# Second layer of a two-layer attention and expert kernel: where the loads of the down weights stand in the queue

## The reference

```python
def _moe(h, w_router, router_bias, w_gate, w_up, w_down):
    shp = h.shape
    hf = h.reshape(-1, shp[-1])
    combine = _route(hf, w_router, router_bias).astype(h.dtype)
    y = jnp.zeros_like(hf)
    for e in range(N_EXPERTS):
        a = jax.nn.silu(hf @ w_gate[e]) * (hf @ w_up[e])
        y = y + combine[:, e:e + 1] * (a @ w_down[e])
    return y.reshape(shp)
```

## Time and profile before

| | |
|---|---|
| median of three runs | 1684.38 us |
| the profiled execution, its own time | 1684.62 us |
| its span, first to last instruction | 1682.6 us |
| TensorE busy | 1587.2 us (94%) |
| VectorE, ScalarE, GpSimd busy | 670.0, 341.5, 123.6 us |
| mean granted clock of TensorE | 0.976 |
| SP's DMA queue: share of the 16 DMA engines over the span | 54.9% |
| bytes read and written | 362.74 and 26.80 MB |

### The profile page before, as it was taken

How to read it: one execution, slowest core, us unless ns; L and a number is a source line. 1 busy time by engine, 2 the same in 40 slices (tenths; PEclk the granted TensorE clock), 3 DMA queues, 4 the chain that set the end, 5 groups by cost and what they waited for, 6 DMA issues and landing times. The chain is left out here.

```text
span 1682.6 us, 16523 instructions
## 1 busy us (share of the span) xinstructions
PE 1587.2 (94%) x6162; PEld 751.8 (45%) x6162; DVE 670.0 (40%) x1608; ACT 341.5 (20%) x782; POOL 123.6 (7%) x193
## 2 busy tenths in 40 slices
PE   5999999999999999899999979999999989998994
PEld 2444456544444445644444434445644445333331
DVE  2430068866677733511100145307867144111113
ACT  1210078820000021110100023007710021000001
POOL 1000000200000010200000020000200100110101
PEclk9999999999999999899999989999999999998998
DMA  9812141115545461699999996222178758999995
GB/s 345 273 50 100 50 168 66 39 51 150 201 151 200 150 225 48 244 349 366 386 391 393 366 355 202 100 100 76 39 227 324 276 193 292 370 388 392 389 360 210
DMA packets 176128, 380.83 MB, mean 226 GB/s; under 512 B 24430, under 2 KB 28670, under 8 KB 175912
## 3 DMA queue, kind: packets, MB, share of 16 engines
q1 hardware_dynamic: 160768, 327.17, 54.9%
q0 software_dynamic: 14272, 50.20, 7.8%
q10 hardware_dynamic: 1008, 2.38, 0.4%
HBM read 362.74 MB, written 26.80 MB: 232 GB/s over the span
## 5 line engine op out<-in xcount | busy, mean ns | idle before, releaser
L1881 PE MATMUL bank<-ring_sb,HT_sb 128*128 128x512 f32 x672 | 298.4, 599 | 3.1 <-ACT HT_sb L847 2.5
L1988 PE MATMUL bank<-ring_sb,HT_sb 128*128 128x512 f32 x544 | 240.6, 595 | 0.0
L1881 PEld LDWEIGHTS bank<-ring_sb,HT_sb 128*128 128x128 f32 x672 | 126.8, 193 | 151.8 <-issue 150.1
L1988 PEld LDWEIGHTS bank<-ring_sb,HT_sb 128*128 128x128 f32 x544 | 102.3, 190 | 135.7 <-issue 135.7
L1992 PE MATMUL bank<-ring_sb,QR_sb 128*128 128x512 f32 x288 | 129.5, 592 | 0.0
L2153 PE MATMUL bank<-ring_sb,HT_sb 128*64 128x512 f32 x480 | 106.5, 596 | 2.8 <-DMA ring_sb<-w_e_up 2.8
L2171 PE MATMUL bank<-ring_sb,QR_sb 128*128 128x512 f32 x208 | 97.8, 626 | 6.5 <-DMA ring_sb<-w_e_down 6.5
L973 ACT ACTIVATE WK_sb<-bank 128x512 f32<-128x512 f32 x36 | 21.5, 597 | 348.6 <-PE bank L1988 348.6
L2134 PE MATMUL bank<-ring_sb,HT_sb 128*128 128x512 f32 x192 | 85.4, 598 | 2.7 <-ACT HT_sb L1007 2.7
L2177 PE MATMUL bank<-ring_sb,QR_sb 128*64 128x512 f32 x304 | 73.8, 630 | 12.6 <-DMA ring_sb<-w_e_down 10.6
L1992 PEld LDWEIGHTS bank<-ring_sb,QR_sb 128*128 128x128 f32 x288 | 54.8, 190 | 68.8 <-issue 68.8
(11 more groups left out here) (336 smaller groups left out, 1708.7 us busy)
## 6 DMA issues: line engine op xcount, KB each, us to landing
ring_sb<-w_e_down SPq DMA_DIRECT2D x32, 2048.0 KB, 17.2
ring_sb<-w_mod SPq DMA_DIRECT2D x24, 2048.0 KB, 9.4
ring_sb<-w_in SPq DMA_DIRECT2D x22, 2048.0 KB, 15.0
ring_sb<-w_e_gate SPq DMA_DIRECT2D x16, 2048.0 KB, 14.8
ring_sb<-w_e_up SPq DMA_DIRECT2D x16, 2048.0 KB, 18.9
ring_sb<-w_e_gate SPq DMA_DIRECT2D x22, 1024.0 KB, 16.4
ring_sb<-w_e_up SPq DMA_DIRECT2D x22, 1024.0 KB, 14.6
ring_sb<-w_branch SPq DMA_DIRECT2D x8, 1024.0 KB, 9.9
```

Of the source, the lines that this page charges most:

```text
L1881: ins = mm(bank[j % 4][:, :], HT[:, k, P * t:P * t + P], WR[slot][:, k], start=(k == 0), stop=(k == KD - 1))
L1988: ins = mm(bank[i % 2][:, :], HT[:, k, P * t:P * t + P], WR[wg][:, k], start=(k == 0), stop=(k == KD - 1))
```

## The change

The down weight of position q - 1 is issued directly behind the pair of position q, from q = 3 on; before, it was the down weight of q - 2, from q = 4 on. Just ahead of the last pair one down weight is issued instead of two. In the first layer both forms give the same list.

```diff
@@ -610,13 +610,11 @@
                 at = [0, 1]
                 for q in range(2, NE):
                     at.append(eng.value_load(order[0:1, q:q + 1], min_val=0, max_val=NE - 1))
-                    lag = 2 if l else 1
                     if q == NE - 1:
-                        for late in range(q - lag, q):
-                            load_expert(l, late, at[late], 2)
+                        load_expert(l, q - 1, at[q - 1], 2)
                     load_pair(l, q, at[q])
-                    if 2 * lag <= q < NE - 1:
-                        load_expert(l, q - lag, at[q - lag], 2)
+                    if 2 + l <= q < NE - 1:
+                        load_expert(l, q - 1, at[q - 1], 2)
                 load_expert(l, NE - 1, at[NE - 1], 2)
```

## The result

The changed kernel takes 1694.60 us (median of seven runs, 1691.48 to 1697.76) against 1685.65 for the kernel before in the same seven rounds (1683.24 to 1687.79). The ratio is 1.0051, 95% interval 1.0039 to 1.0063: slower by 0.5%. The forecast was 1695.4 against a before of 1684.4, +11.0; measured are +8.9 by the medians and +8.6 by the ratio. The profiled execution of the changed kernel lies 1.8 us above its median (1696.37 us, span 1694.4).

What follows compares the result with a forecast made beforehand. The stream of weights was taken to bound the second layer's experts. Hold +10.1, closed hole -3.1 and the tail's +4.1 for D15 gave +11.0 at the last product: 1684.4 + 11.0 = 1695.4 us, range 1689.5 to 1699.

Steps and rivals of the forecast that it cites:

- The bound: Second layer's experts: the full stream of weights is the limit, 388 GB/s from 1439 to 1626 us, not TensorE's waits.
- Part 1: Start of the second layer's experts: SP, held by D2 until 1436.5 us, makes the stream 3.92 MB late, +10.1 us.
- Part 2: After the start: the stream does not stand still again at later waits of SP; costed at nothing.
- The thinnest margin: D3's wait until 1451.69 us: the stream has work until 1456, 4.6 us to spare; if gone, 1 to 2 us.
- Part 3: TensorE's 16.6 us of waits on down weights go, replaced by waits elsewhere; nothing is gained.
- Part 4: The stream's hole from 1626 to 1632 us, behind D14, closes: 1.19 MB, -3.1 us.
- Part 5: Kernel's end: gathers land ahead of D15, which becomes the stream's last load, +4.1 us; last product starts +11.0 us.
- Rival (b): Tail: TensorE's clock falls after longer waits, last product 1.7 to 2.7 us later, 1697.1 to 1698.1 us; chance 0.2.
- (a): Tail: the gathers don't get ahead of D15, so the sum is +7.0, 1691.4 us; chance 0.12.
- (c): The stream stands still again, at 1451.69 us or behind a full position: 3 to 6 us more, 1698 to 1701; chance 0.08.
- (e): Whole kernel: no change, hold and hole in balance, 1684.4 us; chance 0.03.
- (d): SP's hold at the start costs nothing and the closed hole stays: 3.1 us sooner, 1681.3 us; chance 0.05.

Runs made afterwards that it cites:

- run 6: The changed kernel without the second half of the down weights of positions 6 to 9, all matmuls kept: 1685.79 us, ratio to before 1.0001.
- the first load alone: The kernel before, with only the down weight of position 2 moved ahead of the pair of position 4: 1698.07 us, ratio 1.0058.
- run 8: The kernel before, with the pairs of positions 3 and 4 issued as gate, gate, up, up: 1686.54 us, ratio 1.0002.
- run 1: The kernel before in its old order, with only SP's wait for position 0's down product added ahead of position 4's pair: 1695.94 us, ratio 1.0053.
- run 7: The changed kernel, with GpSimd's second-layer gathers held until the last up half has landed: 1692.88 us, ratio to before 1.0044.
- the switch at 6: The kernel before up to position 6's pair, then two down weights, then the changed kernel's order: 1686.00 us, ratio 0.9990.
- the switch at 5: The kernel before up to position 5, there two down weights, then the changed kernel's order: 1687.17 us, ratio 1.0000.

## Why the prediction was right

**The bound.** Right. The stream of weights bounds the second layer's experts, not TensorE: the changed kernel has TensorE 2.5 us less busy and at a higher clock in the long stretch, and it is slower. Leaving out bytes and no matmul gave 8.4 to 8.8 us back (run 6).

**Part 1, the hold of SP.** Right in mechanism and size. +10.1 was forecast. The wait alone costs between 8.9 (ratio) and 10.0 us (medians), the first load alone between 9.8 and 12.1, and the changed kernel has carried 0.32 + 5.78 = 6.10 MB by 1455 us (its windows stand below) against 9.84, so 3.74 MB or 9.6 us at 390 GB/s are missing. One claim beside it was too strong: "nothing can make it up" from 1439 on. The stream of before has some idle time up to about 1445 (run 8), and the windows show it: the lag is 3.90 MB at the end of the first (3.92 was forecast) and 3.74 at the end of the second, where the changed kernel carries 361 GB/s and before 351. The Trainium skill ("DMA: Bandwidth & Descriptors", Anatomy of one DMA) says that any wait on a semaphore happens on the issuing sequencer before dispatch, in a section on GpSimd's path; for SP's queue the windows of run 1 agree, with 12 GB/s in 16.9 us. The figure of 358 GB/s that the same page gives for a core (Specifications) is not what the rows show, 390; it is half of a stack's 716 GB/s, for two cores, and this kernel runs on one.

**Part 2, no further standstill.** Right: 390 GB/s from 1455.46 to 1626.56 in the changed kernel. The thinnest margin held: D3 goes out at 1452.17, and the share is 1.02 from 1439.46 to 1455.46. The windows of the changed kernel, cut as those of run 1:

```profile
1422.56:1439.46 16.90, 16.90 (x54) 7.46 (x54) 2.67 (x4) 1.08 (x2) 0.87 (x2) 1.00 0.07 19
1439.46:1455.46 16.00, 16.00 (x66) 6.35 (x64) 2.39 (x4) 1.19 (x2) 2.20 (x3) 1.00 1.02 361
1455.46:1626.56 171.10, 151.99 (x640) 59.08 (x638) 19.63 (x33) 14.08 (x24) 20.08 (x28) 0.97 1.04 390
```

**Part 3, the waits on down weights.** Right in that they bring nothing. Wrong in "none on down weights", which part of the text on the new profile expected: 9.4 us of waits stay with down weights, in six pieces of at most 2.1 us: TensorE has caught up with the stream and waits for most loads in turn, whichever they are.

**Part 4, the hole.** Right: 6 us x (390 - 190) = 1.2 MB, 3.1 us. In the count from P3 the deficit shrinks from 3.9 MB ahead of the hole's place to 2.7 MB behind it.

**Part 5, the tail.** The term was mis-sized and its picture partly wrong. The gathers were to land ahead of D15, and the sum for it (18 us against 28) counted their issue and left out their landing, which took 6.4 us in the kernel before. In fact the first pair's rows were waited for until 1664.9, 1.8 us ahead of D15: the gathers ran beside D15, each slower than before. How much they took from the stream ahead of the last product is seen from P3's first load to the start of that product, first before, then changed:

```profile
1403.18:1656.62 253.44, 233.42 (x961) 93.80 (x959) 33.05 (x60) 21.27 (x36) 31.76 (x43) 0.95 1.00 369
1403.66:1666.81 263.15, 233.64 (x961) 94.20 (x959) 35.25 (x63) 21.27 (x36) 31.77 (x43) 0.97 0.97 360
```

These are 93.5 and 94.7 MB: 1.2 MB more, 3 us. D15 then cost less than the 4.1 us booked: from 10.1 - 3.1 = 7.0 the start of the last product went to 9.7, so the tail's term is 2.7 (run 7, which moves the gathers back, takes 2.2 of it). The half microsecond booked for the up half, in the middle value, wasn't spent either, because D15 came last by far.

Rival (b), the fallen clock, given 0.2, came true beside it: 1.7 us at the last product, at the lower end of the 1.7 to 2.7 forecast. It struck in two places. In `up_gate(15)` it cost 2.0 us, which D15's landing hides. Before D15, where the wait was 2.95 us, it cost the end 1.7. I had looked at the one place, since I took the last up half and D15 to be 5 to 6 us apart; the half lands 15.7 us after its issue at 1642.18, so they are 8.9 us apart. The last up half's time to landing, as the earlier trace rows:

```profile
ring_sb<-w_e_up SPq DMA_DIRECT2D x1, 1024.0 KB, 15.7
```

Without the fallen clock, 11.0 and 9.7 would be the numbers to set side by side; with it, 11.4 in the profile. The two errors, 1.3 too much and 1.7 too little, nearly cancel, so it is in part luck that the sum came so close.

**The rivals that fell.** (a), the gathers not ahead of D15, came true only in part: the last product starts 9.7 us later, between its 7.0 and the 11.0 of the forecast. Run 7 makes it true by holding the gathers back, and costs 7.5 us at the last product and 7.6 at the additions, close to its 7.0. (c) and (e) did not occur. (d), a free hold and a closed hole, is what the switch at 6 makes true by construction, and even that gained nothing until the gathers were held back as well.

**The size.** The profiles say 11.4 us and the medians 8.9. The profiled execution of the changed kernel was 1.8 us above its kernel's median, and that of before (1684.62) 1.0 below the median of these rounds (1685.65). The 11.4 us and the 0.5 ahead of P3, less 1.8 and 1.0, are 9.1: which executions were profiled makes nearly the whole difference. The runs of the changed kernel spread from 1691 to 1698 us.

## What to carry to other kernels

Where the stream of loads is the bound, count the bytes that it doesn't carry, not the waits of the engine that uses them: a wait in the issuing queue costs nothing while the stream still has issued loads to carry, and where it runs dry, what it would have carried. A load may be moved ahead of others only from the point at which the backlog is longer than the wait it brings along; here that was the sixth position, or the fifth within the noise, and not the third. At the end of the kernel look at what shares the stream with the last weight: transfers that aren't needed sooner can be made to wait for it.

## What the runs showed that I had not expected

Three waits for the last weight of nearly one length cost differently: after 2.95 and 2.99 us the 16 matmuls took 5.35 and 5.34 us, and after 3.00 us, in the run with the switch at 5, they took 6.65. So the clock lost behind a wait isn't a function of its length alone.

```profile
1656.52 6.65 PE L2184 MATMUL bank<-ring_sb,QR_sb 128*64 128x512 f32 x16 [3.00 <-DMA ring_sb<-w_e_down]
```

In the changed kernel TensorE waits more often than before and longer in sum, but for less at a time, and its granted clock is higher in the long stretch, 0.97 for 0.94. Of its 15 waits on weights from 1460 to 1655 us eleven are of 0.6 to 2.1 us, and only one of these cost clock:

```profile
1520.00 8.83 PE L2169 MATMUL bank<-ring_sb,QR_sb 128*128 128x512 f32 x16 [1.81 <-DMA ring_sb<-w_e_down]
...
1624.23 3.65 PE L2175 MATMUL bank<-ring_sb,QR_sb 128*64 128x512 f32 x16 [2.10 <-DMA ring_sb<-w_e_down]
```

The other four, of 2.24 to 2.95 us, cost 1.7 to 2.0 us each. Before, four of the five waits did, 2.8 to 4.8 us long, for 1.7 to 3.0 us each. So a TensorE that waits for nearly every load did lose clock, as rival (b) feared, but less of it than before.
